# A relative-position table laid out by the launch and masked on GpSimd, in place of one made by matmuls and copied through DRAM

## What is computed

```python
def branch_bias(rel_table, dilation, n_keys):
    off, _ = band_offsets()
    bucket = t5_bucket(dilation * jnp.clip(off, 0, n_keys))
    return jnp.transpose(rel_table.astype(jnp.float32)[bucket], (2, 0, 1))
...
def dilated_attention(q, k, v, rel_table):
    outs, lses = [], []
    for window, dilation in DILATED:
        o, l = dilated_branch(q, k, v, rel_table, window, dilation)
        outs.append(o)
        lses.append(l)
    wts = jax.nn.softmax(jnp.stack(lses, 0), axis=0)
    return jnp.sum(wts[..., None] * jnp.stack(outs, 0), 0)
...
def causal_conv(x, w, b):
    S = x.shape[1]
    xp = jnp.pad(x, ((0, 0), (CONV_K - 1, 0), (0, 0)))
    y = b
    for j in range(CONV_K):
        y = y + xp[:, j:j + S] * w[j]
    return y
```

## Time and profile before

| | us |
|---|---|
| median of three runs | 1226.56 |
| the profiled execution, span from the first to the last instruction | 1225.1 |
| TensorE busy | 1191.0 |
| VectorE busy | 538.3 |
| ScalarE busy | 406.5 |
| GpSimd busy | 22.3 |

### The profile page before, as it was taken

One profiled execution on the slowest core, in us unless ns is written; L12 is line 12 of the kernel. 1 busy time (PEld: TensorE's weight loads), 2 busy tenths in 40 slices (PEclk: granted clock), 3 DMA queues, 4 the chain that ended last, 5 costly groups with the idle time before them and its releaser, 6 DMA issues.

```text
span 1225.1 us, 14837 instructions
## 1 busy us (share of the span) xinstructions
PE 1191.0 (97%) x5681; PEld 978.8 (80%) x5681; DVE 538.3 (44%) x841; ACT 406.5 (33%) x664; POOL 22.3 (2%) x39
## 2 busy tenths in 40 slices
PE   8984999999999999999999999999999999999997
PEld 8873888888888777778889888778988888888886
DVE  3403332334325555464578673327533333343335
ACT  4302222223323444443344454434412222133222
POOL 3000000000000000000000000000000000000000
PEclk9996999999999999999999999999999999999999
DMA  8456333333231422224324353103532323323311
GB/s 245 119 61 139 108 96 96 92 104 117 90 103 52 121 61 60 70 87 120 86 67 158 104 163 112 52 32 89 155 103 87 102 87 102 103 93 113 103 35 69
DMA packets 143279, 121.16 MB, mean 99 GB/s; under 512 B 4460, under 2 KB 127396, under 8 KB 143104
## 3 DMA queue, kind: packets, MB, share of 16 engines
q1 hardware_dynamic: 139584, 109.07, 29.9%
q0 software_dynamic: 3648, 11.44, 4.2%
HBM read 115.76 MB, written 4.73 MB: 98 GB/s over the span
## 4 chain that ended last, share of the span: by engine, by line
PE 94%; another core or an unknown queue 3%; DMA 1%; ACT 1%; DVE 1%; issue 0%; POOL 0%; DVEq 0%; SPq 0%; ACTq 0%; POOLq 0%
PE ps L460 28%; PE ps L462 28%; PE ps L461 28%; PE ps L657 2%; PE ps L680 2%; PE ps L895 1%; PE ps L480 1%; PE ps L885 1%; DMA xn<-in_x 1%; PE ps L667 1%; PE ps L758 1%; PE ps L742 1%; PE ps L695 0%; PE ps L867 0%; PE ps L605 0%
## 5 line engine op out<-in xcount | busy, mean ns | idle before, releaser
L1316 DVE TENSOR_TENSOR wlo<-raw,whi 128x1024 fp32r<-128x1024 f32 x200 | 244.8, 1227 | 452.2 <-ACT whi L924 451.3
L460 PE MATMUL ps<-xth,whi 128*128 128x512 f32 (+1 forms) x960 | 367.6, 383 | 22.2 <-DVE wlo L1316 22.2
L462 PE MATMUL ps<-xth,wlo 128*128 128x512 f32 (+1 forms) x960 | 361.0, 376 | 0.0
L461 PE MATMUL ps<-xtl,whi 128*128 128x512 f32 (+1 forms) x960 | 360.7, 376 | 0.0
L924 ACT ACTIVATE whi<-raw 128x1024 fp32r<-128x1024 f32 x200 | 206.4, 1054 | 203.8 <-PE ps L462 141.8
L460 PEld LDWEIGHTS ps<-xth,whi 128*128 128x128 f32 x960 | 181.2, 189 | 56.0 <-DVE wlo L1316 20.8
L461 PEld LDWEIGHTS ps<-xtl,whi 128*128 128x128 f32 x960 | 181.3, 189 | 32.6 <-issue 1.0
L462 PEld LDWEIGHTS ps<-xth,wlo 128*128 128x128 f32 x960 | 181.0, 189 | 32.8
L460 PE MATMUL ps<-whi,hhi 128*128 128x512 f32 x480 | 189.4, 395 | 0.0
L462 PE MATMUL ps<-whi,hlo 128*128 128x512 f32 x480 | 186.9, 389 | 0.0
L461 PE MATMUL ps<-wlo,hhi 128*128 128x512 f32 x480 | 186.8, 389 | 0.0
(11 more groups left out here) (161 smaller groups left out, 927.0 us busy)
## 6 DMA issues: line engine op xcount, KB each, us to landing
raw<-in_ffn_w_gate SPq DMA_DIRECT2D x44, 512.0 KB, 3.8
raw<-in_ffn_w_up SPq DMA_DIRECT2D x44, 512.0 KB, 3.9
raw<-in_ffn_w_down SPq DMA_DIRECT2D x44, 512.0 KB, 3.3
raw<-in_w_in SPq DMA_DIRECT2D x28, 512.0 KB, 3.9
raw<-in_xkv_w SPq DMA_DIRECT2D x16, 512.0 KB, 4.1
raw<-in_w_out SPq DMA_DIRECT2D x8, 512.0 KB, 3.3
raw<-in_xq_w SPq DMA_DIRECT2D x8, 512.0 KB, 4.6
raw<-in_xo_w SPq DMA_DIRECT2D x8, 512.0 KB, 3.3
```

The costliest lines, as they stand in the source:

```text
L460: mm(dst, lh, rh, start=start, stop=False)
L461: mm(dst, lh, rl, start=False, stop=False)
L462: return mm(dst, ll, rh, start=False, stop=stop)
L1316: v.tensor_tensor(wlo[c % SPL][:, :], raw[c % RAW][:, :], whi[c % SPL][:, :].bitcast(F32), ALU.subtract).then_inc(lo_done, 1)
```

## The change

The host builds three inputs: `bias_by_key` (8 x 128 x 512: for each head the finished tile of rel_bias[bucket]), `lnm` (128 x 512: the logs or -1e30) and `conv_cols` (128 x 40: taps and biases of the convolution, already in columns). The matmuls, VectorE's additions, the store, `oh_sb`, `relb`, `crow` and `tb_sb` go; `lnm_sb` becomes a tile of 128 x 512 of its own. GpSimd loads a head's tile, waits for it, adds `lnm_sb` in place and raises `wb_ready`, for which VectorE's first logits of a head wait instead of `wb_in`. The loads of heads 0 and 1 are followed by both additions, then by `g_rows`. The counts of `small_in` fall from 10 loads to 7.

```diff
-            pool.dma_start(crow[0:CK * KT, :], conv_w[0].rearrange("j (c p) -> (j c) p", p=P)).then_inc(small_in, 16)
-            pool.dma_start(crow[CK * KT:, :], conv_b[0].rearrange("(c p) -> c p", p=P)).then_inc(small_in, 16)
-            pool.dma_start(oh_sb[:, :], onehot).then_inc(small_in, 16)
-            pool.dma_start(relb[:, :], rel_bias).then_inc(small_in, 16)
+            pool.dma_start(ccol[:, :], conv_cols).then_inc(small_in, 16)
             pool.dma_start(lnm_sb[:, :], lnm).then_inc(small_in, 16)
...
             load_gb(0)
-            pool.wait_ge(brow_done, 1)
-            pool.dma_start(bias_rows, tb_sb[:, :].unsqueeze(1).to_broadcast([AH, P, DIST])).then_inc(scr_out, 16)
-            pool.wait_ge(scr_out, 16)
+            pool.wait_ge(small_in, 16 * SMALL)
             pool.wait_ge(unit_used, U_VA)
-            for h in range(AH):
+
+            def bias_in(h):
+
                 if h >= 2:
                     pool.wait_ge(lg_done, NB * (h - 1))
-
-
-                src = bass.AP(bias_rows.tensor, h * P * DIST + P - 1, [[DIST - 1, P], [1, S]])
-                pool.dma_start(wb[h % 2][:, :], src).then_inc(wb_in[h % 2], 16)
-                if h == 1:
-                    pool.wait_ge(rows_done, 1)
-                    pool.dma_start(g_rows, grow[:, :]).then_inc(g_out, 16)
+                pool.dma_start(wb[h % 2][:, :], bias_by_key[h]).then_inc(wb_in[h % 2], 16)
+
+            def bias_masked(h):
+
+                pool.wait_ge(wb_in[h % 2], 16 * (h // 2 + 1))
+                nc.gpsimd.tensor_tensor(wb[h % 2][:, :], wb[h % 2][:, :], lnm_sb[:, :], ALU.add).then_inc(wb_ready, 1)
+
+            bias_in(0)
+            bias_in(1)
+            bias_masked(0)
+            bias_masked(1)
+            pool.wait_ge(rows_done, 1)
+            pool.dma_start(g_rows, grow[:, :]).then_inc(g_out, 16)
+            for h in range(2, AH):
+                bias_in(h)
+                bias_masked(h)
...
                 tile(2)
-                if n == 0:
-                    bias_rows_and_conv_columns()
                 with pe.Fori(1, FT // 3) as i:
...
-            down(0, (3, 1, 2, 0), lambda b: pe.wait_ge(*{3: (brow_done, 1), 1: (h_done, FT - 2), 2: (h_done, FT - 1),
-                                                         0: (h_done, FT)}[b]))
+            down(0, (3, 1, 2, 0), lambda b: pe.wait_ge(h_done, {3: 1, 1: FT - 2, 2: FT - 1, 0: FT}[b]))
...
-                if n == 0:
-                    act.wait_ge(scr_out, 16)
                 for k in range(3):
                     split_h(n, k)
...
-                    dve.wait_ge(brow_ready, 1)
-                    step.inc(v.tensor_tensor(tb_sb[:, 0:512], ps[6][0:AH, :], lnm_sb[:, 0:512], ALU.add))
-                    step.inc(v.tensor_tensor(tb_sb[:, 512:DIST], ps[7][0:AH, 0:DIST - 512], lnm_sb[:, 512:DIST], ALU.add))
-                    dve.wait_ge(v_step, step.k)
-                    v.tensor_copy(ccol[:, :], ps[7][:, 256:256 + CK * KT + KT]).then_inc(brow_done, 1)
...
                 if i == 0:
-                    dve.wait_ge(wb_in[h % 2], 16 * (h // 2 + 1))
+                    dve.wait_ge(wb_ready, h + 1)
...
+    bias_by_key = np.ascontiguousarray(np.asarray(inputs['rel_bias'])[bucket].transpose(2, 0, 1))
+    taps = np.concatenate([np.asarray(inputs['conv_w'])[0], np.asarray(inputs['conv_b'])], axis=0)
+    conv_cols = np.ascontiguousarray(taps.reshape(-1, P).T)
```

More of the change, by code:

```diff
@@ L21 @@
 PTS = 5
+SMALL = 7
 def lin(const, per, i):
@@ L54, in macaron_layer @@
 def macaron_layer(nc, x, mem, rel_bias, ln_g, ln_b, w_gate, w_up, w_down, w_in, conv_w, conv_b,
-                  ig_bias, fg_bias, ml_g, w_out, xq_w, xkv_w, xo_w, onehot, lnm, bias_rows, g_rows, out):
+                  ig_bias, fg_bias, ml_g, w_out, xq_w, xkv_w, xo_w, bias_by_key, lnm, conv_cols, g_rows, out):
     S, D = x.shape[1], x.shape[2]
@@ L70, in macaron_layer @@
     CK = conv_w.shape[1]
-    DIST = onehot.shape[1]
     GW = 32 + MH
@@ L135, in macaron_layer @@
         gbias = sb("gbias", [MH, 2])
-        relb = sb("relb", [rel_bias.shape[0], AH])
+        lnm_sb = sb("lnm_sb", [P, S])
         ccol = sb("ccol", [P, CK * KT + KT])
@@ L164, in macaron_layer @@
         hlo = [at(f"hlo{s}", [P, S], hs_at + s * 4 * KB + 2 * KB, F32R) for s in range(SPL)]
-        oh_sb = at("oh_sb", [onehot.shape[0], DIST], hs_at)
-        lnm_sb = at("lnm_sb", [AH, DIST], hs_at + 4 * DIST)
-        tb_sb = at("tb_sb", [AH, DIST], hs_at + 8 * DIST)
         wg_raw = at("wg_raw", [P, KT, GW], hs_at + 12 * KB)
-        crow = at("crow", [CK * KT + KT, P], hs_at + 12 * DIST)
         va = at("va", [P, NB, AW], hs_at)
@@ L224, in macaron_layer @@
         gb_in = sem("gb_in")
-        scr_out = sem("scr_out")
+        wb_ready = sem("wb_ready")
         row_out = sem("row_out")
@@ L246, in macaron_layer @@
         xlo_done = sem("xlo_done")
-        brow_ready = sem("brow_ready")
-        brow_done = sem("brow_done")
         pj_ev = sem("pj_ev")
@@ L591, in rows_block @@
                     last.then_inc(grp_done, 1)
[L593 to L599, removed]
             def warm(count):
@@ L983, in ffn_up @@
                 if n == 0:
-                    act.wait_ge(small_in, 16 * 10)
+                    act.wait_ge(small_in, 16 * SMALL)
                     fn(wg_hi[:, :, :], wg_raw[:, :, :], ACT.Copy).then_inc(wg_hi_done, 1)
@@ L1725, in _, with key_distance_tables @@
             ffn_down(1)
-def key_distance_tables(seq, buckets, max_dist, heads):
+def key_distance_tables(seq, buckets, max_dist):
     import numpy as np
-    d = seq - 1 - np.arange(seq + P)
+    d = (seq - P) + np.arange(P)[:, None] - np.arange(seq)[None, :]
     exact = buckets // 2
@@ L1737, in key_distance_tables @@
     bucket = np.where(d < exact, np.maximum(d, 0), np.minimum(large, buckets - 1))
-    onehot = (np.arange(buckets)[:, None] == bucket[None, :]).astype(np.float32)
     count = np.zeros(d.shape)
@@ L1741, in key_distance_tables @@
         count += (d >= 0) & (d % dilation == 0) & (d // dilation <= window // dilation)
-    row = np.where(count > 0, np.log(np.maximum(count, 1)), -1e30).astype(np.float32)
-    return onehot, np.ascontiguousarray(np.broadcast_to(row, (heads, d.size)))
+    return bucket, np.where(count > 0, np.log(np.maximum(count, 1)), -1e30).astype(np.float32)
 _INS = ['x', 'mem', 'rel_bias', 'ln_g', 'ln_b', 'ffn_w_gate', 'ffn_w_up', 'ffn_w_down', 'w_in', 'conv_w', 'conv_b',
@@ L1756 @@
     arrays, args = {}, []
-    onehot, lnm = key_distance_tables(inputs['x'].shape[1], inputs['rel_bias'].shape[0], 2048,
-                                      inputs['rel_bias'].shape[1])
-    named = [(n, np.ascontiguousarray(inputs[n])) for n in _INS] + [('onehot', onehot), ('lnm', lnm)]
+    bucket, lnm = key_distance_tables(inputs['x'].shape[1], inputs['rel_bias'].shape[0], 2048)
+    bias_by_key = np.ascontiguousarray(np.asarray(inputs['rel_bias'])[bucket].transpose(2, 0, 1))
+    taps = np.concatenate([np.asarray(inputs['conv_w'])[0], np.asarray(inputs['conv_b'])], axis=0)
+    conv_cols = np.ascontiguousarray(taps.reshape(-1, P).T)
+    named = [(n, np.ascontiguousarray(inputs[n])) for n in _INS]
+    named += [('bias_by_key', bias_by_key), ('lnm', lnm), ('conv_cols', conv_cols)]
     for name, a in named:
@@ L1762 @@
         args.append(nc.dram_tensor(f"in_{name}", a.shape, mybir.dt.from_np(a.dtype), kind="ExternalInput").ap())
-    args.append(nc.dram_tensor("bias_rows", (lnm.shape[0], P, lnm.shape[1]), F32).ap())
     args.append(nc.dram_tensor("g_rows", (inputs['ig_bias'].shape[1], inputs['x'].shape[1]), F32).ap())
```

## The result

The changed kernel takes **1228.66 us** (median of 20 runs, 1227.9 to 1231.53); the kernel before, run beside it, 1226.45 us (20 runs, 1225.31 to 1228.54). The ratio is 1.002, with a 95% interval of 1.0013 to 1.0026: slower by 2.2 us, where 23 us less were forecast. The profiled execution spans 1226.8 us, against 1225.1 us before.

A forecast was written before the change was run, and what follows sets the result against it. TensorE's work and its few idle places were taken to bound the kernel. Savings of 20.56, 1.60 and 1.44 us less 0.5 us for start-up gave -23.1 us, from 1226.56 to 1203.5 us; range 1201.0 to 1207.5.

The forecast's parts named there:

- The stall: First FFN: the bias_rows store blocks the weight stream; removing it saves 20.56 us of TensorE gap plus 1.60 us clock recovery.
- the control: Second FFN, same loop without the stall: 232.09 us against 255.90, so weights should keep up once the store goes.
- The three small operations: Between tile 2 and the loop: two small fp32 products and a transpose leave TensorE's path, saving 1.44 us.
- Start-up: Opening loads on full DMA engines: 155 KB more to load, +0.5 us, bounds -0.5 to +2.5 us.
- Masks and their cover: Attention heads: eight GpSimd additions of 1.0 us each (0.5 to 2.0) finish before VectorE needs them, costing 0.
- Contention: GpSimd's masks beside VectorE's work on shared SBUF access: covered, so 0 us.
- rivals B and E: B: masks slow VectorE in attention, 1212.5 us, chance 0.07. E: masks gate the heads, 1242 us, chance 0.02.
- rival D: Something other than the store holds the long weight issue, so the stall stays: 1225.6 us, chance 0.04.

The follow-up runs named there:

- e5: Kernel before, with each table row stored once (20 KB, not 2560) and loads reading one row for all partitions, slant left out: 1204.42 us.
- e7: e1 with 32 bytes of pad ahead of all tiles, the weights' too: 1202.88 us.
- e1: Changed kernel with only the mask's tile allocated last and a 32-byte pad in its old place, all other tiles at their old places: 1203.25 us.
- e15: e1 with only the wlo tiles moved by 32 bytes, and 224 bytes of pad behind so later tiles lie at +256: 1227.46 us.
- e9: e1 with each of GpSimd's eight mask additions replaced by a fill of one column, masking left out: 1203.5 us.
- e2: Changed kernel with 32 bytes of pad behind the mask tile, so later tiles lie 2048 bytes higher and not 2016: 1203.38 us.
- e3: Kernel before, with only a 32-byte pad added behind its bias table relb: 1252.36 us, ratio 1.0207.
- e6: Kernel before, with the table on 128 partitions, each storing its row 8 times, the same 2560 KB as before: 1205.58 us.

## Why the prediction was wrong, point by point

- **The stall (22.16 us) and its cause: right.** All signs asked for are there: no store, issues of 0.37 us, no wait of 20.4 us, a full clock. e5 measures 21.5 us, 22.2 in the stage itself. What was late next: nothing, as the control had said.
- **The three small operations (1.44 us): right**, 1.5 us by e5 against e7.
- **Start-up (+0.5 us): not settled.** The first up product after the last opening transposes starts at 23.55 us and was at 23.47, in e1 at 23.61, so +0.1 us. But each is one execution, and in the other runs' traces the same start lies anywhere from 22.98 (e15) to 25.14 us (e9).
- **Masks and their cover: right.** 1.26 to 1.28 us each from head 2 on against 1.0 taken, within the bound of 2.0; the row for head 2 and VectorE's first use, of the changed kernel:

```profile
441.85 1.28 POOL L422 TENSOR_TENSOR wb<-wb,lnm_sb 128x512 f32<-128x512 f32 x1 [3.58 <-DMA wb<-in_bias_by_key]
```

```profile
453.09 0.29 DVE L1469 SCALAR_TENSOR_TENSOR lg<-ps,wb 128x128 f32<-128x128 f32 x1 [2.31 <-PE ps L645]
```

  The mask is done at 443.13, so 10 us of cover are left, where 11.6 less a mask were predicted; and `lg` waits for TensorE's product, not for `wb_ready`.
- **Contention (0): right** as to the time (e9); rivals B and E did not come.
- **The sum left out a term.** The step that failed is the one that is in no sentence: the start distance of 0.227 us was taken for a property of the matmul and carried over to a kernel in which its operands lie elsewhere. The description of the change even says that `lnm_sb` "becomes a tile of its own". The question to ask was what lies behind it. With the layout held, the forecast of 1203.5 us is 0.3 us off (1203.25); against the kernel before of its own job e1 gains 23.8 us where 23.1 were forecast, so a part of the 0.3 is luck. With the layout moved, 1228.66 - 1203.25 = **+25.4 us** stand against the -23.1, which makes +2.3; +2.2 were measured. The time came near rival D's 1225.6 us, but not by D's mechanism: the store did what the prediction said. No rival had the matmuls themselves change, and so the range was too narrow.

That the layout is the cause is shown (e1, e2, e3, e7); that what counts is the distance between the operands' regions, and that among twelve displacements (0 is one) only the multiples of 256 bytes were fast, is shown for these matmuls. What happens in TensorE or at the SBUF is not shown; e15 gives a hint and a contradiction. That the store from few partitions makes the stall is shown by e5 and e6; how it holds another queue's issue is not.

**The version that beats both** is e1 or e7, the change with its mask tile allocated last: 1203.25 and 1202.88 us, 2% below the kernel before.

## What to carry to other kernels

An edit that adds, drops or resizes an SBUF tile moves every tile behind it, and is a change to the matmuls too: keep the old offsets (allocate new tiles last) or compare the start distance of the commonest matmul before and after, ahead of any other reading. When TensorE's busy time rises while its waits vanish, look into the instructions and not into the schedule. And spread a repeated store over 128 partitions; from 8 it took five times as long and stopped the weight stream.

## What was unexpected of the hardware

- The start distance of an fp32r matmul of 512 columns depends on where its operands lie to each other: 227 ns at the old distance and at 256, 512 or 2048 bytes more, 232 to 234 ns at the others, at a granted clock of 1.00 in the stages compared. Matmuls of 256 columns go the other way, 120 ns against 115 to 119.
- Moving `wlo` by 32 bytes spread the loss over all three matmuls of a group: 232.3, 238.3 and 228.9 ns.
- The store from 8 partitions held an issue of SyncE's queue for 37 to 38 us, though it was on GpSimd's queue; the same bytes from 128 partitions held none. Its packets of 5 KB took 0.79 us each from 8 partitions, 0.23 us from 128.
